# Per-layer embedding moved into the expert loop of a two-layer decoder, expert 23's up weights held whole, hints ahead of TensorE's far branches

## The chip, the core and the metric

The kernel runs on one core of a Trainium2 chip: five engines (TensorE, VectorE, ScalarE, GpSimd, SyncE), each with its own instruction queue, an on-chip memory of 128 partitions (SBUF), eight accumulation banks of 128 x 512 f32 (PSUM) and 16 DMA engines that bring data from HBM. The profile calls the engines PE, DVE, ACT, POOL and SP. The metric is the time of the whole kernel in microseconds on the device, lower is better.

## What is computed

All is in f32, for 256 tokens of width 1024. Layer 0 mixes tokens with a causal convolution module, layer 1 with sparse attention. Behind the mixer each layer has a mixture of 32 experts and a gated embedding:

```
for i in range(DEPTH):
    h = h + mixer_i(rms_norm(h, g_mix[i]))
    h = h + hier_moe(rms_norm(h, g_ffn[i]), ...)            # 32 experts, top-2 of one group
    gate = jax.nn.sigmoid(rms_norm(h, g_ple[i]) @ ple_w_gate[i])
    h = h + gate * (p[i] @ ple_w_proj[i])                   # the per-layer embedding
```

An expert is `(silu(x @ w_gate[e]) * (x @ w_up[e])) @ w_down[e]`, and each of its three matrices has 2,048 KB. The product `p[i] @ ple_w_proj[i]` (256 x 256 by 256 x 1024) depends on inputs alone, so it can stand anywhere ahead of the layer's last step.

## The kernel before

**The expert loop.** `moe(L)` on each engine runs the experts in order, two for each pass of a loop of 16 passes. TensorE gathers the rows of one expert's tokens (32 slots, `gather`, line 612), transposes them (`xg_T`, 618), multiplies by gate and up (`gate_up`, 625), transposes the product of both (`h_T`, 635), multiplies by down (`down`, 642) and adds the result to the tokens' rows in PSUM banks 0 to 3 (`scatter`, 649). An expert with more than 32 tokens gets further rounds: before each expert TensorE loads a count from `tab` and, where it is above zero, branches to a body `surplus_{L}_{s}` that stands behind everything else in TensorE's program, and back to `main_{L}_{s}`. The four surplus bodies are laid down at the very end.

**The ring.** The weights go through `ring`, two slots of 6,144 KB. SyncE issues the loads (`expert`): for expert e the gate and up loads wait until expert e-2's gate and up product is done (`gu_mm`), the down load until its down product is done (`y_mm`). So the DMA queue holds at most what two slots take. Some matrices of experts 16 to 23 are loaded ahead of the loop into memory that lies idle, and VectorE copies them into the ring when their turn comes: gate of 16 in `WB[0]`, up of 17 in `WB[1]`, down of 18 in `WB[2]`, gate of 19 in two halves `HX`, and half of the up weights of 23 in `HU`, columns 2048 to 4095 of `ppw`. The other half of 23's up weights is loaded in the loop (line 338).

**The embedding.** In layer 0 `p` and `ple_w_proj` are loaded into `WB[1]` (lines 384, 385) and the product is made in pieces during the convolution's end and the routing. In layer 1 they are loaded into `ppw` after attention. TensorE transposes `p` (`embeddings_T`, 490) and makes four products (`embedding_product`, 494), ScalarE copies each into `pp`, the lower half of `ppw` (`embedded`, 1184). `WB[1]` can take expert 17's up weights in layer 0 only when all four products are done (`pp_mm`), and in layer 1 `HU` is loaded only after they are done and the first half of expert 0's gate and up product, too (`gu_half`), since `wproj` lies there.

**Routing.** Between the mixer and the loop a chain runs through TensorE (`router_product`, 507), VectorE (lines 1598 to 1627), TensorE (673 to 687), VectorE and TensorE again. It ends with `xg_T` and the copy `xgT_copy` for expert 0. `acc_ok` tells that ScalarE has put h into PSUM (line 1288).

## Time and profile before

| what | us |
|---|---|
| median of three runs | 1298.02 |
| the three runs | 1291.84, 1298.06, 1298.02 |
| the profiled execution | 1299.3 |
| its span | 1297.5 |

The profiled execution lasts 1299.3 us, 1.8 us more than the span that its trace covers. "Busy" is time in which an engine ran an instruction. A row of the chain of waits names the work that released the next step. "issue" is idle time for which the profile shows no cause. PEclk is the clock that TensorE was granted, as a share of full speed: 1.00 is its level of 2.4 GHz, 0.50 that of 1.2 GHz.

### The profile page before, as it was taken

Reading aid. Unit: us, or ns where it says so; the run is one execution under the profiler, and the core shown is the slowest. Engines: PE = TensorE matmul, PEld = TensorE weight load, DVE = VectorE, ACT = ScalarE, POOL = GpSimd, SP = SyncE. Lnnn points to the kernel's source line nnn. Section 1 sums busy time; section 2 is a strip of 40 time slices with the busy share of each in tenths; the row PEclk is TensorE's granted clock in tenths of the full one; section 3 lists DMA queues with packets and bytes.
Section 4 is the critical chain, followed back from the end, with each engine's and each line's share of the span. In section 5 each row is a group of like instructions: output and inputs, shape, how many; then the busy total and the mean of one; then the engine's idle time right before and its main releaser. Section 6 shows DMA issues by size and latency. Waiting matters only on the chain.

```text
span 1297.5 us, 26836 instructions
## 1 busy us (share of the span) xinstructions
PE 1032.6 (80%) x10423; PEld 584.9 (45%) x10424; DVE 316.8 (24%) x891; ACT 299.6 (23%) x707; POOL 447.0 (34%) x739
## 2 busy tenths in 40 slices
PE   7999976777688767679999889867676788767778
PEld 6764643333344334334545555534343345433433
DVE  3984300000121100015046842200000130100111
ACT  5873311111111111112114642211111111111111
POOL 3320354334455343320000220634433455452420
PEclk9999988888888888889999798988888899978989
DMA  9952799999999999999227425799999999997990
GB/s 297 413 191 79 282 430 428 429 428 428 428 429 419 428 428 429 428 405 366 71 65 272 183 106 226 300 429 428 429 428 429 428 427 425 428 428 329 431 387 34
DMA packets 64021, 449.34 MB, mean 346 GB/s; under 512 B 11473, under 2 KB 22345, under 8 KB 38888
## 3 DMA queue, kind: packets, MB, share of 16 engines
q1 hardware_dynamic: 58352, 448.25, 83.6%
q10 hardware_dynamic: 5624, 0.51, 0.3%
q8 instruction: 26, 0.43, 0.1%
q14 instruction: 19, 0.16, 0.0%
HBM read 447.70 MB, written 1.05 MB: 346 GB/s over the span
## 4 chain that ended last, share of the span: by engine, by line
DMA 46%; PE 39%; DVE 6%; ACT 4%; issue 3%; SPq 1%; POOL 0%; ACTq 0%; DVEq 0%
DMA ring<-in_moe_w_up 45%; PE PS L625 14%; PE PS L482 10%; PE PS L602 2%; PE PS L642 2%; ACT arena L1240 2%; PE PS L494 1%; PE PS L807 1%; PE PS L612 1%; PE PS L649 1%; ACT ppw L1240 1%; PE PS L470 1%; DVE ppw L1870 1%; SPq L326 1%; PE PS L507 1%
## 5 line engine op out<-in xcount | busy, mean ns | idle before, releaser
L625 PE MATMUL PS<-ring,arena 128*32 128x256 f32 x4160 | 332.2, 484 | 177.2 <-DMA ring<-in_moe_w_up 173.7
L625 PEld LDWEIGHTS PS<-ring,arena 128*32 128x32 f32 x4160 | 159.0, 134 | 342.5 <-issue 203.7
L1570 DVE TENSOR_TENSOR arena<-PS,arena 64x256 f32<-64x256 f32 x65 | 27.8, 428 | 570.3 <-ACT arena L1308 564.6
L642 PE MATMUL PS<-ring,arena 128*32 128x256 f32 x2080 | 125.7, 381 | 30.8 <-DVE arena L1573 30.8
L1308 ACT ACTIVATE arena<-PS 64x256 f32<-64x256 f32 x64 | 24.2, 377 | 513.7 <-PE PS L625 513.6
L1066 POOL TENSOR_SCALAR arena<-arena 128x32 f32<-128x32 f32 x64 | 18.8, 293 | 291.9 <-PE PS L612 287.5
L1025 POOL TENSOR_SCALAR arena<-arena 128x512 f32<-128x512 f32 x67 | 105.6, 1576 | 19.1 <-POOL arena L1072 12.8
L642 PEld LDWEIGHTS PS<-ring,arena 128*32 128x32 f32 x2080 | 73.1, 109 | 61.1 <-issue 37.4
L1019 POOL TENSOR_SCALAR arena<-arena 128x32 f32<-128x32 f32 x260 | 88.2, 361 | 13.1 <-POOL arena L1066 12.9
L1027 POOL TENSOR_TENSOR arena<-arena 128x512 f32<-128x512 f32 x67 | 85.4, 1275 | 5.6
L612 PE MATMUL PS<-hn,arena 128*32 128x256 f32 x1072 | 75.7, 395 | 7.8 <-issue 7.8
L649 PE MATMUL PS<-arena 32*128 32x256 f32 x1040 | 74.5, 397 | 6.6 <-ACT arena L1306 0.6
L1565 DVE TENSOR_TENSOR arena<-PS,g 128x256 f32<-128x256 f32 x67 | 28.5, 425 | 176.8 <-PE PS L618 176.8
L482 PE MATMUL PS<-wb,xnT 128*128 128x512 f32 x160 | 70.0, 593 | 0.6 <-DVE xnT L1453 0.6
L1072 POOL TENSOR_SCALAR arena<-arena 128x1 f32<-128x1 f32 x64 | 23.1, 360 | 129.2 <-PE PS L649 129.2
L1312 ACT COPY arena<-PS 128x256 f32<-128x256 f32 x64 | 23.9, 373 | 162.9 <-PE PS L642 162.9
L649 PEld LDWEIGHTS PS<-arena 32*128 32x128 f32 x1040 | 50.3, 183 | 17.4 <-issue 17.4
L1014 POOL TENSOR_TENSOR rstd<-rstd,nhalf 128x1 f32<-128x1 f32 x12 | 7.2, 600 | 141.9 <-DVE rstd L1445 141.8
L612 PEld LDWEIGHTS PS<-hn,arena 128*32 128x32 f32 x1072 | 36.4, 109 | 32.8 <-issue 8.7
L1029 POOL TENSOR_TENSOR arena<-arena 128x256 f32<-128x256 f32 x67 | 48.9, 729 | 5.2
L1308 ACT ACT_TABLE_LOAD x32 | 41.1, 1283 | 24.7 <-issue 24.7
L482 PEld LDWEIGHTS PS<-wb,xnT 128*128 128x128 f32 x160 | 30.0, 190 | 36.9 <-issue 36.9
(347 smaller groups left out, 1202.2 us busy)
## 6 DMA issues: line engine op xcount, KB each, us to landing
ring<-in_moe_w_down SPq DMA_DIRECT2D x62, 2048.0 KB, 24.2
ring<-in_moe_w_gate SPq DMA_DIRECT2D x60, 2048.0 KB, 18.4
ring<-in_moe_w_up SPq DMA_DIRECT2D x60, 2048.0 KB, 22.5
wb<-in_ple_w_gate SPq DMA_DIRECT2D x4, 2048.0 KB, 29.9
ring<-in_conv_w_pw SPq DMA_DIRECT2D x3, 2048.0 KB, 18.9
ring<-in_nsa_w_in SPq DMA_DIRECT2D x3, 2048.0 KB, 17.6
wb<-in_moe_w_gate SPq DMA_DIRECT2D x2, 2048.0 KB, 17.4
wb<-in_moe_w_down SPq DMA_DIRECT2D x2, 2048.0 KB, 19.6
```

Of the source, the lines that this page charges most:

```text
L482: i = pe.matmul(PS[:, bank, :], lhs[:, k, t * P:(t + 1) * P], w[:, k, :], start=start and k == 0, stop=(k == KD - 1))
L612: i = pe.matmul(PS[32 * j:32 * j + 32, BGX, 0:Q4].rearrange("q (p c) -> q p c", c=2), lhs[:, t, :], rows[:, j], start=(t == 0), stop=(t == ...
L625: i = pe.matmul(PS[32 * j:32 * j + 32, BGU, 0:256].rearrange("q (p c) -> q p c", c=2), xT[:, k, :], w[:, k, :].rearrange("q (p h c) -> q h ...
L642: i = pe.matmul(PS[32 * j:32 * j + 32, BY, 0:Q4], hT[:, c, 32 * f:32 * f + 32], w_dn(s)[:, f, c, Q4 * j:Q4 * (j + 1)], start=(q == 0), sto ...
L649: i = pe.matmul(PS[:, ACC + j, 256 * t:256 * (t + 1)], w[32 * j:32 * j + 32, t * P:(t + 1) * P], ysb[32 * j:32 * j + 32, :], start=False, ...
L1019: i = g.tensor_scalar(eq4[:, t, k, :], c32, S4[:, t, k:k + 1], None, ALU.is_equal)
L1025: g.tensor_scalar(eqr, srow, cc, None, ALU.is_equal).then_inc(count, 1)
L1027: g.tensor_tensor(eqr, eqr, wrow, ALU.mult).then_inc(count, 1)
L1029: g.tensor_tensor(to, eqr[:, 0, :], eqr[:, 1, :], ALU.add).then_inc(ok, 1)
L1240: i = nc.scalar.copy(xst[c % 2][32 * j:32 * j + 32, q, :], cv0[32 * q:32 * q + 32, c, DVE_TAPS + j:DVE_TAPS + j + XW])
L1308: nc.scalar.activation(gs[64:128, :], PS[0:64, BGU, 0:256], ACT.Silu).then_inc(sil_ok, 1)
L1565: return v.tensor_tensor(dst.rearrange("p (j c) s -> p j c s", c=2), PS[:, BGX, Q4:Q4 + 256].rearrange("p (c j s) -> p j c s", c=2, j=4), ...
```

## The change

The embedding is no longer made ahead of the loop. After expert 23's loads SyncE loads `p` into the first quarter of `xnT` and `ple_w_proj` into the upper half of `ppw`. At the end of pass 13 (behind expert 27) TensorE branches to a new body `embedding_{L}` at the end of its program, which transposes `p`, makes the four products and branches back. VectorE copies the transposes and products out. Expert 23's up weights are loaded whole into `ppw` ahead of the loop, and VectorE copies both halves into the ring. Expert 17's up weights go to `WB[1]` as soon as the bias in it has been used (`hb_ok`). The register `cold_pass` takes the hints out of force in the first pass. The hint for the branch over the far bodies stands behind layer 1's loop and no longer ahead of it.

```diff
+EMB_AT = 14
+EMB_BANKS = (BY, BGU, BHT, BY)
...
-                    if held == 3 and g == 1:
-                        rest = moe_w_up[L, e].rearrange("(p k) f -> p (k f)", k=8)[:, 2048:4096]
-                        sp.wait_ge(hu_ok, L + 1)
-                        sp.dma_start(ring[:, s, 6144:8192], rest).then_inc(gu_in[s], 16)
-                    elif held != g:
+                    if held != g:
                         gate_up_load(L, e, ring[:, s, 4096 * g:4096 * (g + 1)], g, gu_in[s])
...
                 sp.dma_start(HX[0], spare[:, 0:2048]).then_inc(held_in, 16)
-                if L == 0:
-                    sp.wait_ge(pp_mm, 4)
-                    gate_up_load(0, HELD + 1, WB[1], 1, held_in)
-                else:
-                    sp.wait_ge(pp_mm, 8)
-                    sp.wait_ge(gu_half, NE + 1)
-                    sp.dma_start(HU, spare_up[:, 0:2048]).then_inc(held_in, 16)
...
-                pair(m + 3, (None, 3))
+                pair(m + 3, (None, 1))
+                sp.wait_ge(hu_ok, L + 1)
+                sp.dma_start(pin, p[L, 0].rearrange("(t q) d -> q t d", q=P)).then_inc(emb_in, 16)
+                sp.dma_start(wproj, ple_w_proj[L].rearrange("(c p) d -> p c d", p=P)).then_inc(emb_in, 16)
...
             sp.wait_ge(conv_ok, KD)
-            sp.dma_start(HU, up_rest(0)[:, 0:2048]).then_inc(held_in, 16)
+            gate_up_load(0, HELD + 7, ppw[:, :], 1, held_in)
+            sp.wait_ge(hb_ok, 2)
+            gate_up_load(0, HELD + 1, WB[1], 1, held_in)
...
             sp.wait_ge(o_mm, 8)
-            embeddings(1)
             gate_up_load(1, 1, R1[1], 1, gu_in[1])
+            gate_up_load(1, HELD + 7, ppw[:, :], 1, held_in)
...
+            def embedding(L):
+                pe.wait_ge(emb_in, 32 * (L + 1))
+                for c in range(2):
+                    for t in range(NT):
+                        i = pe.transpose(PS[:, 6, (2 * c + t) * P:(2 * c + t + 1) * P], pin[:, t, c * P:(c + 1) * P], ident[:, :])
+                i.then_inc(ptr, 1)
+                pe.wait_ge(pT_ok, L + 1)
+                for b in range(4):
+                    t, n = b // 2, b % 2
+                    if b == 3:
+                        pe.wait_ge(pp_ok, 4 * L + 1)
+                    for c in range(2):
+                        i = pe.matmul(PS[:, EMB_BANKS[b], :], pT2[:, c, t * P:(t + 1) * P],
+                                      wproj[:, c, 512 * n:512 * (n + 1)], start=(c == 0), stop=(c == 1))
+                    i.then_inc(pp_mm, 1)
+                pe.wait_ge(pp_ok, 4 * (L + 1))
+
+            def fillers(count, columns):
+                for _ in range(count):
+                    pe.matmul(PS[:, 0, :], ident[:, :], columns, start=True, stop=True)
...
-            for c in range(2):
-                embedding_product(0, 0, 1, c)
+            fillers(4, dense(PW2[0])[:, 0, :])
...
+                    if s == 0:
+                        hints[L] = (to_surplus, pe.mark_branch_hint_location(cold))
+                    else:
+                        to_surplus.branch_hint(hints[L][1])
+                        hints["embedding"] = pe.mark_branch_hint_location(cold)
...
+                pe.reg_mov(cold, 1)
                 with pe.Fori(0, NE // 2) as it:
                     one_expert(it, 0)
                     one_expert(it, 1)
+                    pe.reg_mov(cold, 0)
+                    pe.br_eq(it, EMB_AT - 1, on_true=f"embedding_{L}", on_false=f"experts_{L}").branch_hint(hints["embedding"])
+                    embed_bb.append(nc.cur_bb)
+                    nc.switch_bb(f"experts_{L}")
+                    hints[L][0].branch_hint(pe.mark_branch_hint_location(cold))
...
-                v.tensor_copy(R1[1][:, 0:2048], HU).then_inc(hu_ok, 1)
-                with dve.Fori(m + 3, NE // 2) as it:
+                v.tensor_copy(R1[1][:, 2048:4096], ppw[:, 2048:4096]).then_inc(hu_ok, 1)
+                v.tensor_copy(R1[1][:, 0:2048], ppw[:, 0:2048]).then_inc(gu_in[1], 16)
+                with dve.Fori(m + 3, EMB_AT) as it:
+                    for s in range(2):
+                        expert_steps(it, s)
+                dve.wait_ge(ptr, L + 1)
+                v.tensor_copy(pT2, PS[:, 6, :].rearrange("p (c q) -> p c q", c=2)).then_inc(pT_ok, 1)
+                for b in range(4):
+                    t, n = b // 2, b % 2
+                    dve.wait_ge(pp_mm, 4 * L + b + 1)
+                    v.tensor_copy(pp[:, t, 512 * n:512 * (n + 1)], PS[:, EMB_BANKS[b], :]).then_inc(pp_ok, 1)
+                with dve.Fori(EMB_AT, NE // 2) as it:
```

The removed steps on TensorE in the routing are best seen as its instructions stand in a row. A row has the line, the operation, what is written and read, and a count. Here is layer 0 from the router's product (`wr`) to the counts' product; before:

```order
L507 MATMUL PS<-wr,xnT 128x36 x16
L494 MATMUL PS<-wb 128x512 x4
L673 MATMUL PS<-iote,ones 128x32
L678 MATMUL PS<-arena,upper 128x32
L673 MATMUL PS<-iote,ones 128x32
L677 MATMUL PS<-arena,ones 128x32
```

and after:

```order
L501 MATMUL PS<-wr,xnT 128x36 x16
L491 MATMUL PS<-hn,ident 128x512 x3
L651 MATMUL PS<-iote,ones 128x32
L656 MATMUL PS<-arena,upper 128x32
L651 MATMUL PS<-iote,ones 128x32
L655 MATMUL PS<-arena,ones 128x32
```

Four embedding products have given way to three fillers. The end of TensorE's loop pass (expert 2·it+1's scatter, then the branch back), before:

```order
L618 MATMUL PS<-ident,arena 128x128 x2
L649 MATMUL PS<-arena 128x256 x8
L769 REGISTER_ALU
L769 COMPARE_AND_BRANCH
L470 MATMUL PS<-ident,h 128x128 x8
```

and after:

```order
L606 MATMUL PS<-ident,arena 128x128 x2
L635 MATMUL PS<-arena 128x256 x8
L753 COMPARE_AND_BRANCH
L756 BRANCH_PREFETCH_HINT
L749 REGISTER_ALU
L749 COMPARE_AND_BRANCH
L456 MATMUL PS<-ident,h 128x128 x8
```

The branch to the embedding body and a hint for the next pass's surplus branch now stand ahead of the branch back. SyncE's queue around expert 23 in layer 0, before:

```order
L326 DMA ring<-in_moe_w_gate 128x4096
L338 DMA ring<-in_moe_w_up 128x2048
L329 DMA ring<-in_moe_w_down 128x4096
L374 UNCONDITIONAL_BRANCH
```

and after:

```order
L326 DMA ring<-in_moe_w_gate 128x4096
L329 DMA ring<-in_moe_w_down 128x4096
L360 DMA xnT<-in_p 128x2x256
L361 DMA ppw<-in_ple_w_proj 128x2x1024
L362 UNCONDITIONAL_BRANCH
```

A load of 1,024 KB has gone from the loop there, and loads of 256 KB and 1,024 KB have come.

## Rows read from the trace of the kernel before

**Rows 1.** The page: the chain's shares; the costliest group, busy, mean ns | idle, releaser.

```profile
DMA 46%; PE 39%; DVE 6%; ACT 4%; issue 3%; SPq 1%; POOL 0%; ACTq 0%; DVEq 0%
L625 PE MATMUL PS<-ring,arena 128*32 128x256 f32 x4160 | 332.2, 484 | 177.2 <-DMA ring<-in_moe_w_up 173.7
```

**Rows 2.** Busy time by stretches: us, engines, PEclk, DMA share, GB/s.

```profile
840.00:1160.00 320.00, 233.90 (x3084) 129.83 (x3080) 36.35 (x75) 39.97 (x80) 142.92 (x243) 0.87 1.01 428
1186.00:1194.00 8.00, 6.80 (x111) 4.03 (x111) 0.72 (x2) 2.41 (x4) 1.02 (x4) 1.00 0.21 53
```

**Rows 3.** The chain of waits in layer 1's loop: start us, us, what.

```profile
1165.75 7.79 issue
1173.54 1.98 PE PS L612 x16
...
1177.27 5.09 PE PS L625 x57
...
1187.83 3.83 PE PS L625 x60
...
1226.19 23.27 DMA ring<-in_moe_w_up
```

**Rows 4.** TensorE in order of time, behind the surplus round.

```profile
1197.12 3.85 PE L625 MATMUL PS<-ring,arena 128*32 128x256 f32 x64
1200.76 1.13 PE L612 MATMUL PS<-hn,arena 128*32 128x256 f32 x16
1207.03 3.83 PE L625 MATMUL PS<-ring,arena 128*32 128x256 f32 x64 [0.56 <-issue]
```

**Rows 5.** The embedding products' line: ns min/median/max, first and last start.

```profile
L494 PE MATMUL PS<-wb x16: 592/592/1201, 84.6 to 140.5; 128*128 128x512 f32 x16
```

**Rows 6.** SyncE's issues in order of time, layer 1.

```profile
819.24 0.33 SPq L364 DMA_DIRECT2D ppw<-in_moe_w_up  x1
819.91 0.33 SPq L367 DMA_DIRECT2D h<-in_moe_w_gate  x1
```

**Rows 7.** The chain of waits from the convolution's end to layer 0's loop.

```profile
95.83 1.73 PE PS L494 x4
97.58 0.59 ACT ppw L1184
...
99.48 0.50 ACT xnT L1256
100.12 22.53 PE PS L602 x48
...
136.21 4.85 PE PS L494 x8
```

**Rows 8.** TensorE by stretches: busy, PEclk, DMA share, GB/s.

```profile
101.00:105.00 4.00, 4.00 (x7) 0.57 0.02 4
802.00:808.00 6.00, 6.00 (x13) 0.52 0.96 408
```

**Rows 9.** VectorE's routing step behind which TensorE's line 678 may start, both layers.

```profile
139.66 0.23 DVE L1619 TENSOR_TENSOR arena<-arena 128x64 f32<-128x64 f32 x1
806.55 0.23 DVE L1619 TENSOR_TENSOR arena<-arena 128x64 f32<-128x64 f32 x1
```

**Rows 10.** TensorE's line 678 in time order, layer 0.

```profile
141.32 0.41 PE L678 MATMUL PS<-arena,upper 128*128 128x32 f32 x2
```

**Rows 11.** TensorE in order of time, layer 1's routing.

```profile
781.17 0.60 PE L490 MATMUL PS<-ident,ppw 128*128 128x128 f32 x4
802.91 6.95 PE L494 MATMUL PS<-ppw,arena 128*128 128x512 f32 x10
810.12 0.41 PE L678 MATMUL PS<-arena,upper 128*128 128x32 f32 x2
814.91 1.13 PE L494 MATMUL PS<-ppw,arena 128*128 128x512 f32 x2
```

**Rows 12.** VectorE's copy of one PSUM bank, in order of time.

```profile
147.38 0.68 DVE L1663 COPY arena<-PS 128x512 f32<-128x512 f32 x1
```

More of the change, by code:

```diff
@@ L569, in _ @@
             taps(KD - 2)
-            pe.wait_ge(pT_ok, 1)
             pe.wait_ge(glu_ok, KD)
-            for c in range(2):
-                embedding_product(0, 0, 0, c)
+            pe.wait_ge(w2_in[0], 16)
+            fillers(2, dense(PW2[0])[:, 0, :])
             pe.wait_ge(ln_acc, 2 * (KD - 4))
@@ L589, in _ @@
             pe.matmul(PS[:, 7, 0:T], ones[:, :], sqb[(KD - 1) % 2], start=False, stop=True).then_inc(lnmm, 1)
-            for c in range(2):
-                embedding_product(0, 0, 1, c)
+            fillers(4, dense(PW2[0])[:, 0, :])
             for t in range(NT):
@@ L619, in xg_T, with gate_up @@
                 return i
-            def gate_up(s, xT, half=False):
+            def gate_up(s, xT):
                 for k in range(8):
@@ L627, in gate_up @@
                                       start=(k == 0), stop=(k == 7))
-                    if half and k == 3:
-                        i.then_inc(gu_half, 1)
                 return i
@@ L651, in scatter @@
                 return i
-            surplus, bodies = {}, []
+            surplus, bodies, hints, embed_bb = {}, [], {}, []
+            cold = pe.alloc_register("cold_pass")
             def moe(L):
                 a = 3 * L + 1
-                if L == 1:
-                    pe.wait_ge(pT_ok, 2)
-                    pe.wait_ge(h_dve, H_DVE[a] - 2)
-                    embedding_product(1, 0, 0, 0)
                 norm_T(a, 1)
@@ L664, in moe @@
                 router_product(L, 1)
-                if L == 1:
-                    embedding_product(1, 0, 0, 1)
-                for n, t in ((0, 1), (1, 0)) if L == 1 else ((1, 0), (1, 1)):
-                    for c in range(2):
-                        embedding_product(L, n, t, c)
+                fillers(3, hn[:, 0, 0:512])
                 pe.wait_ge(const_ok, 2)
@@ L771, in moe @@
                     one_expert(it, 1)
+                    pe.reg_mov(cold, 0)
[3 more added lines that the diff above has]
+                    hints[L][0].branch_hint(pe.mark_branch_hint_location(cold))
+                if L == 1:
+                    hints["end"] = pe.mark_branch_hint_location()
                 norm_T(a + 1, 0)
@@ L980, in _ @@
                         pe.br(f"main_{L}_{s}")
+                with nc.body(f"embedding_{L}", parent=embed_bb[L], valid_engines=[pe.engine]):
+                    embedding(L)
+                    pe.br(f"experts_{L}")
             nc.switch_bb("pe_end")
@@ L1262, in moe @@
                 a = 3 * L + 1
-                if L == 1:
-                    act.wait_ge(ptr, 2)
-                    nc.scalar.copy(pT2[1], PS[:, 4, :].rearrange("p (c q) -> p c q", c=2)).then_inc(pT_ok, 1)
                 xnT_copy(a, ROW_FFN + 8 * L, 0)
```

56 lines of the change are left out of this document (7 added, 49 removed).

## The prediction

> **What bounds the kernel now.** I read the page first, then busy time by stretches, then the chain of waits, then SyncE's issues and single engines in order of time. The chain runs through the DMA for 46% of the span, and TensorE's gate and up product was kept waiting 173.7 us by the landing of the up weights [rows 1]. Between 840 and 1160 us the DMA engines are fully busy at 428 GB/s [rows 2]. At that rate 1,024 KB take 2.45 us and an expert's 6,144 KB take 14.7 us, while TensorE needs 9.3 us for an expert (from 1187.8 to 1197.1) and at most 9.9 [rows 3, 4]. So an expert loop ends when its bytes have landed. Three things move that end: when the uninterrupted stream of loads begins, how many bytes are in it, and whether it ever runs dry. Outside the loops the chain goes through TensorE and VectorE, and time counts there in full.
>
> The stream runs dry once. In layer 1, ahead of expert 26, TensorE goes to the surplus body and stands still for 7.79 us with no cause that the profile knows; then comes the round, and expert 26's own product starts at 1187.83 [rows 3]. From 1186 to 1194 us the DMA moves 53 GB/s, so 8 x (1 - 53/428) = 7.0 us of stream are lost [rows 2]. A delay of 7.8 + 14.3 = 22.1 us (from 1165.75 to 1187.83) thus costs 7.0 us, and a full queue forgives about 15.0 us. The queue's depth fits: up weights land 23.27 us after their issue, of which gate and up themselves take 9.8 [rows 3].
>
> **Convolution's end.** TensorE's first mixer product waits at 100.12 for ScalarE's first SiLU, and that one stands behind the copy of the second embedding product, 0.59 us [rows 7]. Without it the SiLU comes 0.5 us earlier; then VectorE's scaling is next, so no more. Ahead of the wait TensorE had idled 2.6 us, and from 101 to 105 us its clock was granted at 0.57 on average, mostly its level of 1.2 GHz [rows 8]; 24 products took 22.53 us, 0.94 each, while two embedding products at the full 2.4 GHz took 1.73, so 0.87 each [rows 7]. Four fillers of 0.87 now run from 95.8 to 99.3, just short of the SiLU at about 99.5. I take it that the clock stays up: 24 x (0.94 - 0.87) = 1.7 us. Bounds: 0, if the clock falls anyway, to 1.9. VectorE and ScalarE also lose small copies in the convolution; ScalarE's copies of the taps bind there, so I count nothing for them. **Sum 2.2 us.**
>
> **Routing, layer 0.** VectorE releases TensorE's line 678 at 139.9 [rows 9], but TensorE is busy with four products until 141.1 [rows 7] and starts the line at 141.32 [rows 10]. Three fillers from 136.2, the first part at half clock, end near 140.0. **Sum 1.2 us**, bounds 0 and 1.4. Expert 17's up weights leave the routing for the idle stretch before it, which moves neither chain nor stream, since the stream begins only with the loads behind `acc_ok`.
>
> **Bytes, layer 0.** Half of 23's up weights, 1,024 KB, leaves the loop for a DMA that is idle, and 1,280 KB of embedding come: 256 KB more, **0.6 us lost**.
>
> **Start of layer 1.** Four transposes at 781.17 go (0.4 us), and a product ahead of the norm's transposes (0.87, half of it under VectorE's addition: 0.4). Five products at 802.91 become three fillers. The clock there is at 0.52 from 802 to 808 [rows 8], so each filler takes 2 x 0.87 = 1.7 and they end at 808.1 instead of 809.8 [rows 11]: 1.7 us. VectorE would release line 678 at 806.8 [rows 9], 3.3 us ahead of 810.12 [rows 11], and that is the upper bound. Two more products further on, the last at 814.91, held up the row products and `xg_T`: 0.7 us. Expert 0's product starts 3.2 us earlier. The stream began at 819.24 with `HU` and went on with `HX[1]` at 819.91 [rows 6]; the latter now comes at 819.91 - 3.2 = 816.7 and opens it. **2.5 us gained** (bounds 1 and 4).
>
> **Bytes, layer 1.** The stream loses `HU` (1,024 KB) and the loop's other half (1,024 KB), and gains 1,280 KB. `HU` whole is now loaded behind attention, where the queue has idle time. 768 KB less: **1.8 us gained**.
>
> **The hints.** Each pass from the second on names the surplus bodies well ahead of pass 13, so their code should lie at hand. Of the 7.79 us some 1.5 stay (two loads of counts and two branches; an ordinary entry shows 0.56 [rows 4]), 6.3 go. After the gap the clock was low, too: the round's gather took 1.98 instead of 1.13, its gate and up product 5.09 instead of 3.85 [rows 3, 4], together 2.1. Expert 26 is ready 8.4 us earlier, more than the 7.0 of dry stream: **7.0 us gained**, with 1.4 to spare. The bounds are 0 and 7.0. The hints' own price isn't in the trace; with the register move and the new branch it lies between 0 and an ordinary entry's 0.56 for each expert, and TensorE waits for the DMA there, so it costs nothing.
>
> **The embedding body.** Four transposes 0.5, VectorE's copy 0.7 [rows 12] with hand-over, eight matmuls of 512 columns 8 x 0.87 = 6.9, the last copy 0.7: 8.9 us of delay behind expert 27. At half clock (1201 against 592 ns in [rows 5]) it would be 16. In layer 0 a full queue forgives 15.0: nothing. In layer 1 it comes two experts behind the surplus round. Spare 1.4; expert 27 adds 14.7 - 9.3 = 5.4; the next cycle takes 9.9 + 8.9 - 14.7 = 4.1; 2.7 us are left, so again nothing, but this is the thin place: at half clock it would cost 4.4. VectorE's added copies (five of a PSUM bank, 0.7 us each [rows 12], and one of 2048 columns in SBUF) lie in time in which it waits for TensorE and the DMA.
>
> **Sum.** Layer 0: 2.2 + 1.2 - 0.6 = 2.8. Layer 1: 2.5 + 1.8 + 7.0 = 11.3. Together 14.1 us off the profiled 1299.3, 1285.2. The median is 1298.0, so 1283.9.
>
> **A rule against it.** The row shows a 7.79 us halt on the way out to the surplus body and none on the way back: its scatter is followed at once by main's product at 1187.83 [rows 3]. The Trainium skill, in "Runtime: NRT & Kernel Launch", section "Instruction fetch mechanics", says that prefetch is purely sequential and that a taken branch to code outside the current two-page window has to fetch it before going on. By that rule a body at the program's end is fetched at each visit; the trace agrees on the way out and not on the way back. The page says nothing of hints. What it would give is the third and the fourth case below.
>
> **The rivals.**
> (1) The forecast, chance 0.46: 1283.9, its own range 1280 to 1288.
> (2) The hint does nothing for the surplus branch, but the embedding's body is at hand. For it: hint and surplus branch of slot 0 stand only a few instructions apart, so if nothing is kept between passes there is no lead. Layer 1 keeps its 7.0 us of dry stream; behind it the spare is 5.4 - 4.1 = 1.3, so the embedding is still free. 1283.9 + 7.0 = 1290.9. Chance 0.25.
> (3) Every first visit to far code halts, the embedding's too, by 6.3 us. Layer 0: 8.9 + 6.3 = 15.2, about the 15.0 forgiven. Layer 1: 1.3 - 6.3, so 5.0 us dry beside the 7.0 that stay. 1290.9 + 5.0 = 1295.9, no change. For it: the halt in the trace. Against it: 13 passes of hints. Chance 0.12.
> (4) Slower: the far code drives the loop's own code out, so that the way back from the embedding halts, too. The detour is 8.9 + 12.6 = 21.5 us. Layer 0 runs dry for 21.5 - 15.0 = 6.5, layer 1 for 12.6 - 1.3 = 11.3: 1290.9 + 6.5 + 11.3 = 1308.7. It is slower than before as soon as the two halts make more than about 9 us. Against it: the free way back in the trace. Chance 0.07.
> (5) The small gains fail (clock at the convolution's end, routing under fillers at half clock), the hint works: 1283.9 + 1.7 + 1.2 + 1.5 = 1288.3. Chance 0.10.
>
> **Range and chances.** 1280 to 1296 takes in (1), (2), (5) and most of (3), and leaves out (4), some of (3) and tails. Half a per cent (6.5 us) is about what a measurement of this kernel can tell from no change; 1291.5 is its lower edge, close above (2), of which I give two thirds to faster. Faster 0.46 + 0.17 + 0.06 = 0.69, no change 0.22, slower 0.09.
>
> **What the profile after would show.** Convolution's end: granted clock 1.00 from 100 to 105, 24 products in 20.9 us. Routing: line 656 starts within 0.3 us of VectorE's release in layer 0, 1.7 us later than it could in layer 1. Layer 1's stream starts with one load of 1,024 KB, 2.5 us earlier against the end of attention. Surplus: a halt of 1 to 2 us instead of 7.79, no stretch below 400 GB/s between 1180 and 1200. Embedding: about 9 us between expert 27's scatter and 28's product, with no DMA gap behind it. The prediction is wrong if a halt over 5 us stands ahead of the surplus round or the embedding, or if TensorE halts behind the loops' ends, where the code now follows a hinted branch that was not taken.

## The result: slower by 0.8%, the surplus halt shorter and dearer halts elsewhere

| what | before | after |
|---|---|---|
| median, us | 1297.38 | 1308.66 |
| lowest and highest, us | 1291.84, 1301.49 | 1298.03, 1323.05 |
| profiled execution, us | 1299.3 | 1307.6 |
| its span, us | 1297.5 | 1305.8 |

The ratio is 1.0083 (95% interval 1.0067 to 1.0099), some 11 us more where 14 less were forecast, outside the range of 1280 to 1296. Runs over 1.5% above the fastest of the same kernel (1323.05 here, 1316.81 in e1) are left out of the ratios. The times also scatter more than before. First comes the page of the kernel after: the chain's shares, the costliest group, TensorE's standstills without a known cause by line (sum, count, longest), and the queue that brings TensorE's code (packets, MB, share).

```profile
PE 45%; DMA 37%; DVE 7%; issue 6%; ACT 4%; SPq 1%; POOL 0%; ACTq 0%; DVEq 0%
L613 PE MATMUL PS<-ring,arena 128*32 128x256 f32 x4160 | 312.2, 461 | 150.0 <-DMA ring<-in_moe_w_up 135.4
PE PS L600 <- issue: 27.8, 5, 7.9
PE PS L613 <- issue: 13.3, 11, 3.1
PE PS L628 <- issue: 10.1, 3, 5.4
q8 instruction: 61, 1.00, 0.3%
```

Against [rows 1] TensorE waits less for up weights (135.4 us, was 173.7), DMA's share of the chain has fallen from 46 to 37% and "issue" has doubled from 3 to 6%. The last row of the page of before reads otherwise:

```profile
q8 instruction: 26, 0.43, 0.1%
```

So 35 more packets of 16 KB were fetched in this queue. I take it for TensorE's, since its count changes in the runs below while only TensorE's loop code differs. Where it stood still is seen in the chain of waits of layer 1's loop (start us, us, what), where [rows 3] had 7.79 us at 1165.75:

```profile
1164.09 2.11 issue
1166.20 1.75 PE PS L600 x16
...
1199.51 0.60 PE PS L476 x4
1200.13 0.70 DVE xnT L1679
1200.88 7.15 PE PS L484 x16
1208.05 0.70 DVE ppw L1683
1208.75 2.40 issue
1211.15 5.34 PE PS L613 x58
...
1236.50 0.90 PE PS L600 x12
1237.40 5.55 issue
1242.95 1.07 PE PS L600 x4
1244.02 0.44 PE PS L621 x2
1244.49 0.30 DVE arena L1538
1244.93 3.63 PE PS L628 x32
...
1254.22 0.18 PE PS L600
1254.40 6.79 issue
1261.19 1.93 PE PS L600 x15
```

The surplus halt fell to 2.11 us, and the embedding's body (L476, L484) is entered at once. But TensorE now halts in pass 15, in the middle of the gather that stands in the steps of expert 30 and of expert 31, after 12 and after 1 of its 16 products, for 5.55 and 6.79 us, and its clock falls: the down product takes 3.63 us instead of 1.93. The same two halts stand in pass 1 of layer 1 (5.44 us at 841.12 and 7.89 us at 857.99, after the same 12 and 1 products); in layer 0 there are two, in L628. Between two such places lie 121 matmuls (4 + 2 + 32 + 2 + 16 + 64 + 1) and as many weight loads, besides waits and branches, so I read them as borders of pieces of code. This is the loop's own code, which had been at hand in the passes between.

That these two halts cost in full is seen from the end of the stream, TensorE and DMA in two stretches (us, TensorE busy, PEclk, DMA share, GB/s), first before, then after:

```profile
1258.00:1260.00 2.00, 2.00 (x34) 1.00 1.05 385
1262.00:1264.00 2.00, 1.53 (x9) 1.00 0.65 239
```

```profile
1258.00:1260.00 2.00, 0.00 (x0) 0.67 0.50 182
1260.00:1262.00 2.00, 0.81 (x8) 0.50 0.03 5
```

The stream ends 4 us earlier than before, while TensorE's last scatter comes at 1268.30 instead of 1260.24. The bytes were there; TensorE wasn't. The last halt (1254.40 to 1261.19) also goes on after the weights' stream has ended, so it doesn't last that long merely because the DMA is busy. One dry stretch stands behind the embedding in place of the one of [rows 2]:

```profile
1184.00:1194.00 10.00, 9.22 (x148) 5.63 (x141) 1.15 (x3) 1.12 (x3) 5.30 (x10) 1.00 1.00 410
1214.00:1220.00 6.00, 5.40 (x90) 3.11 (x82) 0.72 (x2) 0.75 (x2) 1.97 (x6) 0.98 0.69 254
```

It loses 6 x (1 - 254/428) = 2.4 us, against 7.0 before.

### The profile page after: what moved, and what is told of

Same layout as the page of the kernel before. It is cut to its first block, busy times and chain, and to the rows that moved or that the text cites. A ratio compares the mean times of both kernels' runs of the same rounds, so it can differ in the third digit from the quotient of the medians.

```text
span 1305.8 us, 27047 instructions
## 1 busy us (share of the span) xinstructions
PE 1038.7 (80%) x10447; PEld 587.7 (45%) x10448; DVE 325.5 (25%) x902; ACT 294.8 (23%) x698; POOL 450.4 (34%) x739
## 4 chain that ended last, share of the span: by engine, by line
PE 45%; DMA 37%; DVE 7%; issue 6%; ACT 4%; SPq 1%; POOL 0%; ACTq 0%; DVEq 0%
DMA ring<-in_moe_w_up 37%; PE PS L613 16%; PE PS L468 10%; PE PS L628 4%; PE PS L600 2%; PE PS L590 2%; PE PS L635 2%; ACT arena L1222 2%; PE PS L484 1%; PE PS L794 1%; ACT ppw L1222 1%; PE PS L456 1%; PE PS L606 1%; DVE ppw L1845 1%; SPq L326 1%
## 5 line engine op out<-in xcount | busy, mean ns | idle before, releaser
L613 PE MATMUL PS<-ring,arena 128*32 128x256 f32 x4160 | 312.2, 461 | 150.0 <-DMA ring<-in_moe_w_up 135.4
L628 PE MATMUL PS<-ring,arena 128*32 128x256 f32 x2080 | 136.5, 400 | 41.0 <-DVE arena L1538 30.9
L628 PEld LDWEIGHTS PS<-ring,arena 128*32 128x32 f32 x2080 | 75.7, 113 | 77.3 <-issue 55.3
L600 PE MATMUL PS<-hn,arena 128*32 128x256 f32 x1072 | 80.6, 406 | 27.8 <-issue 27.8
L1013 POOL TENSOR_TENSOR arena<-arena 128x512 f32<-128x512 f32 x67 | 85.8, 1280 | 5.6
```

The source lines that it names most:

```text
L600: i = pe.matmul(PS[32 * j:32 * j + 32, BGX, 0:Q4].rearrange("q (p c) -> q p c", c=2), lhs[:, t, :], rows[:, j], start=(t == 0), stop=(t == ...
L613: i = pe.matmul(PS[32 * j:32 * j + 32, BGU, 0:256].rearrange("q (p c) -> q p c", c=2), xT[:, k, :], w[:, k, :].rearrange("q (p h c) -> q h ...
L628: i = pe.matmul(PS[32 * j:32 * j + 32, BY, 0:Q4], hT[:, c, 32 * f:32 * f + 32], w_dn(s)[:, f, c, Q4 * j:Q4 * (j + 1)], start=(q == 0), sto ...
L1013: g.tensor_tensor(eqr, eqr, wrow, ALU.mult).then_inc(count, 1)
```

## The experiments

Two theories stood at first. **Theory A:** hints in force fetch far code, and this pushes out the loop's own. **Theory B:** the visit to the embedding's body pushes it out. Theory names K, L, V and so on in the expectations are explained there. Times are compared by ratio to the kernel before, run beside; the halts are those of one profiled execution of each, in us, and those under 1.4 us are left out. "Embedding back" is the halt on the way back from the embedding's body. Most kernels have 9 to 12 runs, e7 and e10 five and e9 six.

| kernel | ratio (95%) | code packets | surplus in | embedding in, L0/L1 | embedding back, L0/L1 | other halts in the loops |
|---|---|---|---|---|---|---|
| before | 1 | 26 | 7.79 | | | |
| after | 1.0083 (1.0067 to 1.0099) | 61 | 2.11 | 0/0 | 3.04/3.14 | 4.57, 5.37; 5.44, 7.89, 5.55, 6.79 |
| e1 | 1.0050 (1.0014 to 1.0086) | 29 | 8.12 | 5.29/6.65 | 2.91/2.63 | |
| e2 | 0.9989 (0.9966 to 1.0011) | 38 | 1.97 | | | 4.87; 4.94, 6.30, 1.70, 6.76 |
| e3 | 1.0013 (0.9990 to 1.0036) | 30 | 7.71 | 0/0 | 2.95/2.79 | |
| e4 | 1.0034 (1.0009 to 1.0059) | 44 | 2.10 | 5.43/0 | 3.20/3.15 | 5.11, 4.90; 5.52, 7.10, 6.38 |
| e5 | 0.9988 (0.9973 to 1.0002) | 26 | 7.45 | | | |
| e6 | 0.9997 (0.9979 to 1.0014) | 34 | 2.17 | 0/0 | 2.94/2.78 | 5.52 behind the surplus round |
| e7 | 1.0052 (1.0016 to 1.0087) | 46 | 7.74 | 2.94/0 | 4.87/4.86 | 2.6 to 2.8 at the start of ten passes |
| e8 | 1.0020 (1.0001 to 1.0040) | 34 | 7.62 | 5.21/0 | 3.04/2.85 | 5.12; 5.44, 6.52 |
| e9 | 1.0076 (1.0056 to 1.0096) | 29 | 6.91 | 5.70/5.57 | 2.94/2.73 | |
| e10 | 1.0148 (1.0126 to 1.0169) | 28 | 6.83 | 5.05/5.94 | 2.61/2.69 | |
| e11 | 1.0037 (1.0021 to 1.0053) | 29 | 8.07 | 0/0 | 2.95/2.78 | |
| e12 | 1.0000 (0.9987 to 1.0013) | 27 | 6.99 | | | |
| e13 | 0.9993 (0.9973 to 1.0014) | 31 | 7.59 | | | 2.70 |
| e14 | 0.9982 (0.9959 to 1.0006) | 36 | 2.06 | | | 5.11; 4.86, 1.76, 6.29 |
| e15 | 1.0000 (0.9982 to 1.0018) | 28 | 7.51 | | | 1.5 at the start of some passes |
| e16 | 0.9975 (0.9960 to 0.9989) | 30 | 2.07 | 0/0 | 3.91/3.86 | 1.7 at the start of some passes |
| e17 | 1.0058 (1.0038 to 1.0078) | 34 | 2.14 | 0/0 | 3.94/3.87 | 6.43 behind the surplus round; 1.8 as e16 |
| e18 | 0.9997 (0.9975 to 1.0018) | 32 | 7.86 | 0/0 | 3.90/3.90 | 1.7 to 1.8 as e16 |

### The hints taken apart: e1 to e4

e1 (e1_no_loop_hints) is the changed kernel without the three hints; e3 (e3_embedding_hint) keeps the embedding's alone, e4 (e4_surplus_hints) the two surplus hints alone; e2 (e2_before_surplus_hints) puts these two into the kernel before.

```diff
-                    if s == 0:
-                        hints[L] = (to_surplus, pe.mark_branch_hint_location(cold))
-                    else:
-                        to_surplus.branch_hint(hints[L][1])
+                    if s == 1:
                         hints["embedding"] = pe.mark_branch_hint_location(cold)
...
-                    hints[L][0].branch_hint(pe.mark_branch_hint_location(cold))
```

> The changed kernel without the three hints in TensorE's loop and without their register; the hint for the last branch stays. Theory A (the hints' fetches push the loop's own code out): the instruction queue falls from 61 packets to about 26 to 30, the halts in the middle of an expert's products (4.57, 5.37, 5.44, 7.89, 5.55 and 6.79 us) are gone, the surplus round is preceded by 7 to 8 us again, and the embedding's body by 5 to 8 us at its first visit in each layer. Time about 1295 (1291 to 1298). Theory B (the visit to the embedding's body pushes the loop's code out, whatever is hinted): the halts near each loop's end stay, packets stay above 45, time 1303 or more.

> The kernel before with the two hints for the surplus branches in each pass (off in the first), the embedding where it was. Theory A: over 35 packets in the instruction queue instead of 26 and halts of 4 to 8 us inside the loop, though no embedding body is there; the halt ahead of the surplus round falls from 7.8 to about 2. Time 1296 to 1306, by where the halts fall. Theory B: 26 to 28 packets, no halt in the loop, the surplus halt gone, time about 1291.

> The changed kernel with the embedding's hint alone in the loop. Theory A in its form that each kind of hint costs by itself: some halts of 4 to 8 us in the loop stay, packets between 28 and 61, surplus halt back at 7 to 8 us, none ahead of the embedding; 1295 to 1305. If only hints that take turns (two or more targets) push code out: no halts inside, about 28 packets, about 1291.

> The changed kernel with the two surplus hints alone in the loop. Theory A: more than 35 packets and halts inside the loop, surplus halt about 2 us, a halt of 5 to 8 us ahead of the embedding; 1298 to 1308. Theory B: as the changed kernel near the loops' ends, 1303 or more, but no halts in the loop's first passes.

e2 has no embedding in its loop and halts in it all the same, for 4.87, 4.94, 6.30 and 6.76 us; e3 has the embedding and does not. e4 halts, e1 does not. So theory A holds and B falls: with the surplus hints in force the loop's own code goes, embedding or not. In order of time, TensorE of e2 (in brackets the idle time before and what ended it):

```profile
851.43 0.64 PE L625 MATMUL PS<-ring,arena 128*32 128x256 f32 x2 [4.94 <-issue]
868.29 1.50 PE L625 MATMUL PS<-ring,arena 128*32 128x256 f32 x11 [6.30 <-issue]
1170.19 1.12 PE L612 MATMUL PS<-hn,arena 128*32 128x256 f32 x16 [1.97 <-issue]
1188.97 0.42 PE L625 MATMUL PS<-ring,arena 128*32 128x256 f32 x2 [1.70 <-issue]
1216.10 0.64 PE L625 MATMUL PS<-ring,arena 128*32 128x256 f32 x2 [6.76 <-issue]
```

The surplus halt of 7.79 us became 1.97, but 1.70 and 6.76 us came behind it: 10.4 us in all. In e2 they fall in time in which TensorE waits for the DMA, and the time can't be told from before. (Its profiled execution needs 436.6 us from layer 1's first expert product to the last scatter, before 443.2, so there the gap in the stream was won back nearly in full; its ten runs allow 4.4 us less at most. Why they show less than this one profile stays open.) In the changed kernel the halts meet the embedding's detour and the loop's end. Against e3 the two surplus hints cost 1.0083 - 1.0013 = 0.7%, 9 us, where -7.0 was forecast; the two were not run side by side, and the intervals leave some 4 us either way.

The four combinations tell more than that. Without the embedding's hint the surplus hints cost nothing that can be told: e4 against e1 is 1.0034 against 1.0050, e2 is 0.9989. The loss comes with all three. The packets say the same: e1 has 29, the embedding's hint adds 1 (e3), the surplus hints add 15 (e4), all three together add 32. In e4 the last halt in the loop (6.38 us, at 1221.98) stands in expert 28's step, four experts from the end, and no halt over 1.1 us stands in pass 15:

```profile
1228.36 1.07 PE L600 MATMUL PS<-hn,arena 128*32 128x256 f32 x4 [6.38 <-issue]
```

With the embedding's hint added, two stand in pass 15. The embedding's hint does open the way in: without it (e1) the body is entered with 5.29 and 6.65 us. That e1 takes 0.4% more than e3 lies within the two intervals.

### What the embedding and the rest are worth: e5, e6, e11

e5 (e5_no_body) leaves out the embedding's computation and keeps its loads:

```diff
-                    pe.br_eq(it, EMB_AT - 1, on_true=f"embedding_{L}", on_false=f"experts_{L}").branch_hint(hints["embedding"])
-                    embed_bb.append(nc.cur_bb)
-                    nc.switch_bb(f"experts_{L}")
```

> The changed kernel without any hint in the loop, without the branch to the embedding and without the embedding's transposes, products and copies; its two loads stay, so the bytes are those of the changed kernel. The output lacks the embedding. Theory D (the detour costs: it stands two experts behind the surplus round, where the queue has not recovered, and its own halts make it 15 us instead of 8.9): against the kernel with the embedding's hint alone (1299.8) the dry stretch of about 3 us near 1218 us and the low clock behind it go, and in layer 0 some 1 to 2 us; 1293 to 1296. The surplus halt stays at 7 to 8 us. Rival B (the bytes and the stream's start are what failed, the detour is hidden): within 1.5 us of 1299.8.

By medians 1.0013 - 0.9988 = 0.25%, 3.2 us, lie between e3 and e5, as theory D had it, though the two were not run side by side and their intervals overlap. Two stretches of TensorE and DMA show where: behind the embedding e3 runs dry and e5 doesn't.

```profile
1214.00:1224.00 10.00, 9.29 (x132) 0.90 0.85 323
```

```profile
1214.00:1224.00 10.00, 7.85 (x103) 0.83 1.00 428
```

10 x (1 - 323/428) = 2.5 us. But e5 says more: with the embedding gone altogether, with no hints and the byte counts of the changed kernel, the time is only 1.6 us below that of before (0.9988; 3.5 below to 0.3 above). All gains of the prediction other than the hints were to make 7.1 us. In the profile they are in their places (expert 0's product in layer 0 at 143.99 instead of 148.09) and thinner at the end (span 1293.1, 4.4 us less).

e6 (e6_at_15) sets `EMB_AT = 15` in e3.

> The changed kernel with the embedding's hint alone, and the embedding behind expert 29 (EMB_AT = 15) instead of 27. Theory D: two more experts give the queue 2 x 5.4 us of recovery, so the dry stretch behind the embedding goes, but then only two experts are left and TensorE is 15 - 10.8 = 4 us late at the loop's end: about even, 1298 to 1301. Rival N (a detour hidden anyway, the time lies elsewhere): 1299.8 +- 1 with the same dry stretches as before. What tells them apart is the dry stretch behind the body: none by D, though the time is alike.

The dry stretch behind the body is gone as expected (428 GB/s from 1236 to 1246 us, 415 in the next 10 us), and the time lies in the range expected. What was not expected is the surplus: entered with 2.17 us though no hint names it, and then 5.52 us of halt at main's product, on the way back. The sum is 7.7, as in e3, in another place.

e11 (e11_no_fillers) is e3 without its nine `fillers`.

> The changed kernel with the embedding's hint alone and without its nine fillers (2 and 4 at the convolution's end, 3 in each routing). Theory F (the fillers keep TensorE's clock up, as the prediction had it): granted clock near 0.57 again behind 100 us, the 24 products of the mixer's output take 1.7 us longer, the router's follow-up in layer 0 is at half clock; 1.5 to 2.5 us above 1299.8. Rival G (the clock would have stayed up or fallen anyway and the fillers only stand in the way in the routing): 0 to 2 us below 1299.8.

Theory F holds for the clock and these products; the whole time is 0.24% above e3's, within the two intervals. Here are a piece of the chain and a stretch, first of e11, then of the kernel after:

```profile
99.29 22.54 PE PS L588 x48
101.00:105.00 4.00, 4.00 (x7) 0.62 0.02 8
```

```profile
98.01 20.84 PE PS L590 x48
101.00:105.00 4.00, 4.00 (x11) 1.00 0.01 4
```

With fillers the clock stays at its full level, and the products take 1.70 us less, as forecast. This is the firmest result here: the 24 products take 20.84 us in the profiled execution of all 13 kernels with fillers and 22.36 to 22.54 in the seven without.

### How long a hint lasts: e8, and hints in force once: e12, e15, e7, e9, e10

e8 (e8_second_pass) keeps all three hints in force in the second pass alone (slot 0's already at the end of the first).

```diff
-                    pe.reg_mov(cold, 0)
+                    pe.reg_alu(cold, it, 0, ALU.not_equal)
```

> The changed kernel, with all three hints in force in the second pass alone. Theory K: nothing is kept over eleven passes. Packets of TensorE's code fall from 61 to 32 to 36, the halts within products go except perhaps one in the pass behind the hints, the surplus halt is back at 7 to 8 us and the embedding is entered with 5 to 7 us: as without hints, 1302 to 1308. Rival S (far code once fetched stays at hand, as the prediction had it): surplus halt near 2, embedding under 1, no halts in products, 1290 to 1296.

The halts within products stand right behind the hinted pass (5.12 us in layer 0; 5.44 and 6.52 us at 846 and 864 us in layer 1) and then never again, and the surplus halt is back at 7.62 us: nothing fetched in pass 1 was at hand in pass 13, and the halts at the end of the kernel after came from the later hints. Only the entry in layer 1's embedding is free against the expectation.

e12 (e12_before_armed) puts into the kernel before one hint, in force only if the next pass's first expert has a surplus:

```diff
+                    if s == 1:
+                        pe.reg_alu(none_next, pe.value_load(flat[0:1, bass.ds(it * 2 + 2, 1)], min_val=0, max_val=64), 0, ALU.is_equal)
+                        hints[L].branch_hint(pe.mark_branch_hint_location(none_next))
+                    else:
+                        hints[L] = to_surplus
```

> The kernel before, with one hint for slot 0's surplus branch at the start of slot 1's product, about 14 us ahead of that branch, in force only where the coming expert has a surplus (once in the run). This is the prediction's term 'the hints' alone. Theory K with lead (the code must be fetched once, early enough, and is then not thrown out): packets of TensorE's code 26 to 28, no halts in products, surplus halt 2 us instead of 7.8, no dry stretch at 1186 to 1194: 7.0 us less, 1290 to 1292. Rival L (the far code takes the place of the loop's own, so what the way out saves comes back as a halt of 5 us on the way back): time as before, 1296 to 1299, halt moved behind the round. Rival Z: no effect of the hint, halt 7.7 in the same place.

There are 27 packets, the surplus halt is 6.99 us, and the time is that of before: rival Z. In e7 (e7_armed), where slot 0's armed hint stands at the pass's end and slot 1's behind slot 0's branch, it does no more for the surplus (7.74), and the added loads of counts go with new halts of 2.6 to 2.8 us at the start of ten passes, which nothing here explains.

> The changed kernel, with the surplus hints in force only where the coming expert has a surplus (the hint's register is computed from the count in tab), so once in the whole run; the embedding's hint as it was. Theory K (each hint in force fetches the far code anew and pushes out the loop's own, which halts later): 30 to 34 packets of TensorE's code instead of 61, no halt within the products of passes 1 to 12, surplus halt about 2.1 us, embedding entered without halt; 6 us less than with the embedding's hint alone where the stream ran dry: 1294 to 1297. Rival P (a hint instruction costs by being there, in force or not): halts within products as in the changed kernel, 1303 or more.

e9 (e9_armed_early) and e10 (e10_armed_at_15) put e12's hint right behind the embedding's in the code, in the changed kernel, with the embedding behind expert 27 and 29:

> The changed kernel with the embedding's hint in each pass as it was and the one armed hint for slot 0's surplus of the run before, none for slot 1. Theory K with lead: surplus halt 2 us, no halts in products, embedding entered freely; TensorE comes to the embedding 6 us earlier than with the embedding's hint alone (1299.8), so both the 7 us of dry stream at the surplus and the 3 us behind the embedding shrink: 1292 to 1295. Rival L: the loop's own code halts behind surplus or embedding, 1297 to 1301.

> As the run before with the embedding behind expert 29 (EMB_AT = 15). Where theory K holds this has no dry stretch at all, but two experts to catch up at the end: 1291 to 1295, within 1.5 us of the run before. By rival L 1297 to 1301.

Both expectations failed. The embedding was entered with 5.05 to 5.94 us, as if it had no hint, and e10's time was the worst of all. In e18 the embedding's hint stands alone in slot 1; the armed hint stands at slot 0's start and names slot 1's branch, and the entry is free. The reading that fits is that of two hints with no branch between them the second takes the first out of effect, even where its own register holds it back. It isn't shown alone: in e9 and e10 a load of a count stands between the two hints as well, and the armed hint names another branch than in e18.

### Which surplus hint does the work, and the best version: e13 to e18

e13 (e13_slot1_hint) and e14 (e14_slot0_hint) put one of the two surplus hints into the kernel before.

```diff
+                    hints[L].branch_hint(pe.mark_branch_hint_location(cold))
```

> The kernel before with slot 1's surplus hint alone, in each pass from the second; hint and branch have no other branch between them. Theory V (a hint is void once another branch is passed, so only this one fetches; the two bodies lie next to each other, so it serves slot 0's branch too): 32 to 40 packets of TensorE's code, halts of 5 to 7 us within products in passes 1 and 2, surplus halt 2 us; 1295 to 1298 as with both hints. Rival W (both hints work alike): as the other run of this pair.

> The kernel before with slot 0's surplus hint alone, in each pass, ahead of the loop's branch back. Theory V: void, 26 to 27 packets, no halts in products, surplus halt 7.0 to 7.8 us, 1297 to 1299. Rival W (both hints work alike): 32 packets or more, surplus halt 2 us, halts in products.

Theory V falls: slot 0's hint, ahead of the loop's branch back, is the one that both shortens the surplus halt (2.06) and brings the halts in the loop (5.11, 4.86, 1.76, 6.29), with 10 more packets. Slot 1's serves a branch that is never taken here, brings 5 packets, and leaves the surplus halt (7.59) and the time as they were; one halt of 2.70 us stands in the loop. So slot 1's hint does nothing for slot 0's body, though the bodies lie next to each other. From the surplus round on e14 halts for 2.06 + 1.76 + 6.29 = 10.1 us, against 7.79 in one piece before.

e15 (e15_armed_slot1) moves the armed hint to the start of slot 0 and onto slot 1's branch, in the kernel before; e16 (e16_armed_slot1_after) does so in the changed kernel, with `EMB_AT = 15` and the embedding's hint in slot 1.

```diff
+                    if s == 0:
+                        pe.reg_alu(none_next, pe.value_load(flat[0:1, bass.ds(it * 2 + 2, 1)], min_val=0, max_val=64), 0, ALU.is_equal)
+                        hints[L] = pe.mark_branch_hint_location(none_next)
+                    else:
+                        to_surplus.branch_hint(hints[L])
+                        hints["embedding"] = pe.mark_branch_hint_location(cold)
```

> The kernel before with slot 1's surplus hint in force only where the next pass's slot 0 has a surplus, so once, at the start of expert 24's product, 30 us ahead of the surplus round. Theory V with one fetch: 27 to 30 packets, halts in products at most once and behind the hint, surplus halt 2 us, no dry stretch or one of under 3 us: 1290 to 1294. Rival L (the fetch pushes out the loop's code, which halts about as long as is saved, on the way back or in the pass before): 1296 to 1299. Rival Z (a hint in force for the first time does nothing): surplus halt 7 us, 26 to 27 packets, 1297 to 1299.

> The changed kernel with the embedding behind expert 29, the embedding's hint in each pass, and the armed hint of the run before; no other surplus hint. Theory V with one fetch: surplus halt 2 us, embedding entered freely, 1291 to 1296. Rival L: 1298 to 1304.

e15 is rival Z: 7.51 us and no change. But its hint names slot 1's body while the surplus is slot 0's, and by e13 that one wouldn't have helped in each pass either; only e12 and e7 put the armed hint on the branch that is taken. e16 is the one version of 18 whose interval lies below the kernel before, by 0.25% (0.9975; 0.9960 to 0.9989). Its chain behind expert 25:

```profile
1165.12 2.07 issue
...
1181.73 0.60 issue
...
1234.54 3.12 issue
```

To tell hint from chance, e17 (e17_never_armed) holds e16's surplus hint back for good, every instruction in its place (`-1, ALU.not_equal` for `0, ALU.is_equal`), and e18 (e18_armed_at_14) is e16 with `EMB_AT = 14`.

> The run e16 (embedding behind expert 29, the embedding's hint in each pass, one surplus hint) with the surplus hint's register always non-zero, so that it is never in force; the instructions are the same. Theory H (the armed hint did it): surplus halt 7 us, or 2 us with 5.5 us on the way back as in e6, the stream dry for about 7 us, 1298 to 1301. Rival C (the hint did nothing; which code is at hand at the surplus depends on what was fetched before): surplus halt 2 us and no halt on the way back, 1294 to 1297 as e16.

> The run e16 with the embedding behind expert 27, as the changed kernel has it. Theory H: surplus halt 2 us, dry stretch there 3 us, embedding entered freely and 3 us of dry stream behind it, 1295 to 1298. Rival C: nothing is promised by the hint; surplus halt 7.7 us as in e3, 1299 to 1301.

e17, the same stretch:

```profile
1168.38 2.14 issue
...
1185.06 6.43 issue
...
1246.43 3.13 issue
```

It takes 1.0058, 0.8% more than e16 by ratio, and the halt on the way back is there again as in e6. So the armed hint did not shorten the way out, which is 2.1 us either way; with it the way back was free. Of the 13.6 us between the two profiled spans 9.5 arise in layer 1's loop and 3.3 ahead of layer 0's, where the two kernels are alike. In e18, with the embedding two experts earlier, neither happens: 7.86 us on the way out, nothing on the way back, and the time of before. Neither H nor C is right as it was put.

## Why the prediction was wrong, step by step

**The hints (-7.0 forecast, the step that failed).** Its first half came true: the surplus halt fell from 7.79 to 2.11 us, the gap in the stream at 1186 to 1194 us closed. What failed is the sentence on the hints' own price, "between 0 and an ordinary entry's 0.56 for each expert", so "it costs nothing". I looked for the price at the hint and it stands elsewhere. With the hints in force the loop halts for 4.6 to 7.9 us within its own code, and more code is fetched; e2 and e14 show this without any embedding. That the fetched code takes the place of the loop's own is the reading that fits. Six such halts stand in the kernel after. Four fall in a full queue and are forgiven (the DMA keeps 424 to 429 GB/s around them); the last two (5.55 + 6.79, with some 3.4 us of half clock behind) come when the stream is about over. Bounds of 0 and 7.0 for the term left out a loss, with the mechanism written down under rival (4), "the far code drives the loop's own code out", and priced there for the embedding's way back alone. Against e3 the term measured about +9 us; without the embedding's hint (e2 against before, e4 against e1) it measured about nothing. So the sum also left out what the hints do to one another.

**The embedding body (0 forecast).** The body took 1199.51 to 1208.75, 9.2 us (8.9 forecast), entered without a halt, as forecast; 2.4 us of halt on the way back were rival (4)'s. The spare was put at 2.7 us; the detour took more, and 2.4 us of stream went. e3 against e5 gives about 3 us for it by ratio, within their intervals, so this term is mis-sized. Without the embedding's hint it would be some 5 us more by e1, which the intervals don't settle either.

**Convolution's end (-2.2) and layer 0's routing (-1.2).** Right. The clock is 1.00 behind 101 us (0.57 in [rows 8]), 24 products take 20.84 us (22.53 in [rows 7]), line 656 starts at 136.75, 4.6 us earlier than line 678 in [rows 10], and expert 0's product at 145.11 instead of 148.09. Two details of this execution are off. Line 656 starts 1.0 us behind VectorE's release (135.74) and not within 0.3, since the three fillers ran partly at half clock (4.35 us); in e3 it starts at once, at 136.75 behind 136.70. And the clock was low again behind 138 us (L665 took 1.82 us instead of 1.13). One profiled execution isn't enough for such terms: expert 0's product starts at 146.4 to 150.9 (median 148.5) in the six kernels with the old code ahead of the loop and at 143.6 to 148.7 (median 144.3) in the 13 with the new one and fillers. That is 4.1 us for 3.4 forecast.

**Bytes, layer 0 (+0.6).** Not separable. In e5 the loads start 4.2 us earlier (`HX[1]` issued at 146.50, before 150.66), and the last expert's product starts 2.6 us earlier (568.92, before 571.48) and takes 1.1 us longer, its clock having fallen. From 2.8 forecast for layer 0, 1.4 were left there, and in the kernel after it came to 4.0 us more than before (last scatter 585.23, before 581.27). Its last product waited for the DMA until 574.99, 6 us later than in e5; the dip behind the embedding (382 GB/s from 540 to 550 us) explains 1.1 of them, and the rest stays open.

**Start of layer 1 (-2.5) and its bytes (-1.8).** Right: against the attention's first output product (770.96, 3.6 us later than before), expert 0's product came 0.7 us earlier (816.37, before 817.09), so 4.3 us were gained where 3.2 were forecast, and `HX[1]` opens the stream at 818.97. From layer 0's last scatter to this product the six kernels with the old code have 235.8 to 236.5 us, the 13 with the new one 231.0 to 236.1, median 232.6: 3.2 us less, but in some nothing. The stream ended 4 us earlier than before though layer 1 began 4 us later. In e5 layer 1 as a whole gained 3.0 us against the end of layer 0, where 4.3 were forecast.

**The sum.** Layer 0: 6.8 us worse than forecast, layer 1: 15.6 us worse. By the ratios of the runs the surplus hints account for about 16 us (9 against -7.0), the embedding's detour for 3, the small gains for 5 (e5: 1.6 of 7.1), each with some 3 to 4 us of doubt. Why the small gains stand in the traces and hardly in the runs stays open.

**The rivals.** (1) to (3) and (5) are out. (4) gave 1308.7 and 1308.66 was measured, but it had the right number by partly wrong terms: it had the hint do nothing at the surplus and two halts of 6.3 us about the embedding. That it hit the number is luck. What was measured is its mechanism, set off by the hints. It had a chance of 0.07 because of one row, the free way back from the surplus round. e6 and e17 show what that row is worth: with another history the same way back halts for 5.5 to 6.4 us. **Half a per cent** is also what to say of the experiments: the intervals of e2, e3, e5, e6, e12 to e15 and e18 take in no change, and e4, e8, e11 and e16 lie less than half a per cent from it.

## What to carry to other kernels

A hint for a far branch isn't priced at the hint: it brings code in, and here the loop of over 528 instructions then halted within its own code, so count the code packets of the profile before and after and look for standstills within products. Price a standstill by where it falls: the same 5 to 7 us were free in the middle of a loop that waits for the DMA and cost in full, with the clock behind them, in the last two experts. When a row speaks for a free way back, ask for a trace of a kernel that fetched other code before it before giving the rival 7 in 100.

## What the runs showed of the hardware

- The kernel before ran 10,423 matmuls and 10,424 weight loads on TensorE; 32 passes of 264 and 264 are in it. What is executed once is thus 20,847 - 30 x 528 = some 5,000 instructions and control, 190 or more for each of the 26 packets of 16 KB that were fetched. So a loop of more than 528 instructions stayed at hand over all 16 passes: there are no packets to fetch it again in each.
- A halt ahead of the surplus body is 6.8 to 8.1 us where its code is not at hand, one ahead of the embedding's 5.0 to 6.7 (2.9 in e7), one on the way back from it 2.6 to 4.9. Halts within the loop's products are 4.6 to 7.9 us; four shorter ones were 0.69 (e4), 1.70 (e2), 1.76 (e14) and 2.70 (e13).
- Six filler products in idle time kept the granted clock at 1.00 from 101 to 105 us, where the seven kernels without them have 0.57 to 0.89, and saved 1.70 us on the next 24 products (e11).
- With a second hint behind the embedding's and no branch between them, the embedding's had no effect (e9, e10: 5.1 to 5.9 us of halt; e18: none).
- Slot 0's surplus hint in force in each pass kept its body's code at hand (e14: 2.06 us); in force once, 14 us ahead, it did not (e12: 6.99 us), nor right ahead of the branch (e7: 7.74 us), and slot 1's hint did not in either way (e13, e15: 7.59 and 7.51 us).
